# RWKV chunk inverses with exchanged halves on four quadrants, and two LayerNorms centred by the mean of seven tiles ahead of the eighth

## The reference

```python
def _layernorm(x, g, b):
    xf = x.astype(jnp.float32)
    mu = jnp.mean(xf, axis=-1, keepdims=True)
    var = jnp.mean(jnp.square(xf - mu), axis=-1, keepdims=True)
    y = (xf - mu) * lax.rsqrt(var + NORM_EPS) * g.astype(jnp.float32) + b.astype(jnp.float32)
...
    def step(S, inp):
        r_t, w_t, k_t, v_t, a_t, b_t = inp
        sa = jnp.einsum('bhij,bhj->bhi', S, a_t)
        S = S * w_t[:, :, None, :] + sa[..., None] * b_t[:, :, None, :] + v_t[..., None] * k_t[:, :, None, :]
        y = jnp.einsum('bhij,bhj->bhi', S, r_t)
        return S, y
```

## Time and profile before

| | |
|---|---|
| time, median of 3 runs | 2090.66 us (2089.09 to 2099.26) |
| time of the profiled execution | 2087.72 us |
| its span | 2085.9 us |
| PE busy | 1970.8 us (94%), 17574 instructions |
| DVE busy | 1509.0 us (72%) |
| ACT busy | 912.9 us (44%) |
| POOL busy | 516.6 us (25%) |
| RWKV units 0 to 3 begin on PE at | 205.95, 245.13, 294.49, 340.62 us |
| second norm: last residual begins, first scaled tile | 1206.92, 1226.26 us |
| third norm: last residual begins, end of the span | 2062.38, 2085.9 us |

### The profile page before, as it was taken

The page is one execution under the profiler, slowest core; times in us unless marked ns, Lnnn a source line. Parts: engine busy times, 40 slices in busy tenths (PEclk is TensorE's granted clock), DMA queues, the critical chain, the costliest instruction groups (busy, mean ns, idle before and its releaser), DMA issues.

```text
span 2085.9 us, 42823 instructions
## 1 busy us (share of the span) xinstructions
PE 1970.8 (94%) x17574; PEld 1609.5 (77%) x17574; DVE 1509.0 (72%) x2103; ACT 912.9 (44%) x1540; POOL 516.6 (25%) x419
## 2 busy tenths in 40 slices
PE   7999898899999999999999979999989999999997
PEld 6787777777885656655579958888767799999885
DVE  3366665468994677688869866888884789898844
ACT  3325543344324444444465365555443544343423
POOL 2553221140005999300001121111111111111000
PEclk9999999999999999999999989999999999999998
DMA  9222344332452222112138858999964433333321
GB/s 366 86 92 71 124 144 144 145 133 74 157 191 92 71 91 86 61 64 79 66 136 327 294 217 236 311 305 303 323 206 167 142 102 102 103 104 114 137 91 41
DMA packets 127507, 317.89 MB, mean 152 GB/s; under 512 B 12129, under 2 KB 59105, under 8 KB 120913
## 3 DMA queue, kind: packets, MB, share of 16 engines
q1 hardware_dynamic: 114048, 248.65, 35.7%
q0 software_dynamic: 10672, 53.14, 7.0%
q10 hardware_dynamic: 2592, 13.37, 1.6%
HBM read 238.69 MB, written 76.41 MB: 151 GB/s over the span
## 4 chain that ended last, share of the span: by engine, by line
PE 78%; DVE 10%; issue 4%; ACT 4%; DMA 3%; POOL 1%; SPq 1%; ACTq 0%; POOLq 0%; DVEq 0%
PE psum L524 15%; PE psum L3785 14%; PE psum L2017 7%; PE psum L3209 5%; PE psum L2983 5%; PE psum L2640 5%; PE psum L2603 3%; PE psum L1196 3%; PE psum L2615 2%; PE psum L3379 2%; PE psum L337 2%; PE psum L3438 1%; PE psum L3329 1%; PE psum L2691 1%; PE psum L3185 1%
## 5 line engine op out<-in xcount | busy, mean ns | idle before, releaser
L3209 PE MATMUL psum<-h,u_w 128*128 128x256 f32 (+1 forms) x768 | 157.5, 349 | 7.3 <-DVE h L3137 5.2
L524 PE MATMUL psum<-h_split,in_w 128*128 128x512 f32 x600 | 139.1, 391 | 1.5 <-POOL in_w L513 1.5
L3209 PEld LDWEIGHTS psum<-h,u_w 128*128 128x128 f32 x768 | 118.0, 190 | 27.1 <-issue 10.9
L3742 POOL TENSOR_TENSOR ring<-ring 128x1024 f32<-128x1024 f32 x16 | 54.1, 3383 | 319.1 <-DVE xT L3736 319.1
L524 PEld LDWEIGHTS psum<-h_split,in_w 128*128 128x128 f32 x600 | 111.8, 188 | 27.3 <-ACT prev L860 2.1
L513 POOL TENSOR_TENSOR u_w<-ring,u_w 128x512 fp32r<-128x512 f32 x42 | 53.9, 1283 | 276.2 <-ACT u_w L501 240.9
L506 DVE TENSOR_TENSOR w_split<-ring,w_split 128x512 fp32r<-128x512 f32 x54 | 40.4, 748 | 86.3 <-ACT w_split L501 85.9
L2017 PE MATMUL psum<-x_high,ring_split 128*128 128x512 f32 x272 | 101.1, 393 | 0.0
L2640 PE MATMUL psum<-area,ckv_tm 128*128 128x512 f32 (+1 forms) x256 | 100.4, 545 | 0.0
L2738 DVE TENSOR_REDUCE early<-psum 128x1 f32<-128x768 f32 (+1 forms) x96 | 74.8, 780 | 32.2 <-PE psum L2615 29.6
L513 POOL TENSOR_TENSOR in_w<-ring,in_w 128x512 fp32r<-128x512 f32 x50 | 77.4, 1548 | 79.2 <-ACT in_w L501 77.0
(11 more groups left out here) (530 smaller groups left out, 5247.0 us busy)
## 6 DMA issues: line engine op xcount, KB each, us to landing
ring<-in_s_glu SPq DMA_DIRECT2D x64, 512.0 KB, 3.3
ring<-in_w_mod SPq DMA_DIRECT2D x48, 512.0 KB, 5.4
c_pow<-made_c_pow SPq DMA_DIRECT2D x32, 576.0 KB, 5.1
ring<-in_s_in SPq DMA_DIRECT2D x32, 512.0 KB, 6.7
b_pow<-made_b_pow SPq DMA_DIRECT2D x15, 1024.0 KB, 10.5
ring<-in_w_in SPq DMA_DIRECT2D x25, 512.0 KB, 3.3
table<-made_table SPq DMA_DIRECT2D x32, 384.0 KB, 6.6
made_c_pow<-area POOLq DMA_DIRECT2D x10, 1152.0 KB, 5.7
```

Of the source, the lines that this page charges most:

```text
L524: ins = nc.tensor.matmul(out, rounded(buffer(u, w)[:, ks]), values(x, k), start=(first and k == 0 and n == 0), stop=(last and k == UNIT_K ...
L3209: ins = nc.tensor.matmul(o, rounded(u_w[:, u % 4, w, kk * P:(kk + 1) * P]), h3_part(x, k)[:, a:a + size], start=(k == 0 and n == 0), stop= ...
L3742: nc.gpsimd.tensor_tensor(left_plain(i, "S3"), left_plain(i, "A11"), left_plain(i, "S3"), ALU.subtract).then_inc(pool_done, 1)
```

## The change

Two parts. In RWKV, `Z` and `AT` (and so `AL`) are kept with the halves exchanged: the products that make them go to half `1 - odd`. `U` then comes out in the natural half, the step of `Z` in the exchanged half and the step of `ZT` in the natural one, and `dz_pe` issues the two in pairs instead of one after the other. `X(e)` and `Y(e)` become banks `2e` and `2e + 1`. `ZT` no longer comes from `AT`: a new product `at_natural_pe` makes the matrix once more in the natural half, and `zt0_dve` masks it out of PSUM. `akt_pe`, which uses the same bank, follows when that mask is done. At level 2 ACT copies `UA` in two instructions instead of one.

In `ln2` and `ln3` the mean of tiles 0 to 6 (`first_mean_pe`) is formed inside the last tile's products, tiles 0 to 6 are centred by it and squared ahead of tile 7, and tile 7 is centred by it too. What is left of the mean is then the sum of the centred tile 7 over 1024 (`rest`), so the variance is the mean square less the square of `rest`, and each tile gets `rest` subtracted (`rest_dve`, `rest_pool`, "whole") ahead of its scaling. For `ln2` DVE does all 8, for `ln3` GpSimd does two. The first S5 projection of tile 0 multiplies the high part with both weights before it waits for the low part.

```diff
+            def first_mean_pe(self, pe):
+                pe.wait_ge(*at(self.name, "z_sum", KD - 3))
+                self.ones_product(self.mean_bank, self.stat[:, 1, :], True, False)
+                pe.wait_ge(*at(self.name, "z", KD - 2))
+                self.ones_product(self.mean_bank, self.z[:, KD - 2, :], False, True).then_inc(pe_done, 1)
+                pe_count.up(self.name, "first_mean")
...
+            def last_var_pe(self, pe):
+                pe.wait_ge(*at(self.name, "centred", KD - 1))
+                self.quarters_pe(self.rest_bank, self.z[:, KD - 1, :], True, True).then_inc(pe_done, 1)
+                pe_count.up(self.name, "rest_quarters")
+                self.ones_product(self.mean_bank, self.z[:, KD - 1, :], True, True).then_inc(pe_done, 1)
+                pe_count.up(self.name, "rest")
+                pe.wait_ge(*at(self.name, "sq", KD - 1))
+                self.quarters_pe(self.var_bank, self.sq[:, KD - 1, :], False, True).then_inc(pe_done, 1)
+                pe_count.up(self.name, "var")
...
+            def rest_dve(self, dve, k):
+                dve.wait_ge(*at(self.name, "rest_kept"))
+                nc.vector.tensor_tensor(self.z[:, k, :], self.z[:, k, :], self.rest, ALU.add).then_inc(dve_done, 1)
+                dve.wait_ge(dve_done, dve_count.up(self.name, "whole", k))
...
         def X(e, a=0, n=TT * CHUNK):
-            return bank(e, a, a + n)
+            return bank(2 * e, a, a + n)
 
         def Y(e, a=0, n=TT * CHUNK):
-            return bank(2 + e, a, a + n)
+            return bank(2 * e + 1, a, a + n)
...
-                product_pe(b, 0, lhs, rhs).then_inc(pe_done, 1)
+                product_pe(b, 0, lhs, rhs, crossed=True).then_inc(pe_done, 1)
...
+        def at_natural_pe(pe, q):
             for e in range(2):
                 pe.wait_ge(*at("rw", q, "Z0", e))
                 pe.wait_ge(*at("rw", q, "RBT_masked", e))
+            product_pe(0, 0, b_cm, a_cm).then_inc(pe_done, 1)
+            pe_count.up("rw", q, "AT_natural")
+
+        def akt_pe(pe, q):
+            for e in range(2):
+                pe.wait_ge(*at("rw", q, "ZT_masked", e))
             product_pe(0, 0, k_cm, a_cm).then_inc(pe_done, 1)
...
-                if level < LEVELS:
-                    turns(e, 0, lambda h, tt: ZZ[h, 1, tt, :], lambda h, tt: UA[h, 0, tt, :])
-                turns(e, 256, lambda h, tt: UA[h, 0, tt, :], lambda h, tt: ZZ[h, 1, tt, :]).then_inc(pe_done, 1)
+                for tt in range(TT):
+                    if level < LEVELS:
+                        crossed_turn(2 * e, 0, tt, lambda h, tt: ZZ[h, 1, tt, :], lambda h, tt: UA[h, 0, tt, :])
+                    ins = turn(2 * e + 1, 256, tt, lambda h, tt: UA[h, 0, tt, :], lambda h, tt: ZZ[h, 1, tt, :])
+                ins.then_inc(pe_done, 1)
...
-            akt_pe(pe, i)
+            at_natural_pe(pe, i)
             if scan:
                 state_pe(pe, i - 1, 1)
+            akt_pe(pe, i)
...
-            for m in range(1, KD):
+            for m in range(1, KD - 1):
                 mla_out_steps_pe(pe, m, 0, KE)
+            mla_out_steps_pe(pe, KD - 1, 0, KD)
+            ln2.first_mean_pe(pe)
+            mla_out_steps_pe(pe, KD - 1, KD, KE)
...
                 ln2.scale_dve(dve, k)
                 if k == 2:
                     lags_dve(dve, 0)
+                if k + 3 < KD:
+                    ln2.rest_dve(dve, k + 3)
...
+                    if m == KD - 1 and unit == 1:
+                        ln3.first_mean_pe(pe)
```

More of the change, by code:

```diff
@@ L364, in build, with __init__ @@
         class LayerNorm:
-            def __init__(self, name, z, tokens, sq, stat, gain, shift, eps_col, mean_bank, var_bank):
+            def __init__(self, name, z, tokens, sq, stat, gain, shift, eps_col, mean_bank, var_bank, rest_bank=None, rest=None, by_pool=0):
                 self.name, self.z, self.tokens, self.sq, self.stat = name, z, tokens, sq, stat
@@ L403, in mean_pe, with quarters_pe, first_var_pe @@
                 pe_count.up(self.name, "mean")
+            def first_mean_pe(self, pe):
[4 more added lines that the diff above has]
+                pe_count.up(self.name, "first_mean")
+            def quarters_pe(self, b, src, start, stop):
+                for q in range(4):
+                    ins = nc.tensor.matmul(bank(b, 0, self.quarter)[32 * q:32 * q + 32, :], mask("ones")[:, 0:32],
+                                           src[:, self.quarter_of(q)], start=start, stop=stop)
+                return ins
+            def first_var_pe(self, pe):
+                for k in range(KD - 1):
+                    pe.wait_ge(*at(self.name, "sq", k))
+                    self.quarters_pe(self.var_bank, self.sq[:, k, :], k == 0, False)
+            def last_var_pe(self, pe):
[7 more added lines that the diff above has]
+                pe_count.up(self.name, "var")
             def var_pe(self, pe):
@@ L418, in spread_pe @@
                 pe.wait_ge(*at(self.name, "rate"))
+                if self.rest is not None:
+                    pe.wait_ge(*at(self.name, "rest_kept"))
                 edge = self.tokens - T
@@ L456, in scale_dve @@
             def scale_dve(self, dve, k):
+                if self.rest is not None and k >= KD - self.by_pool:
+                    dve.wait_ge(*at(self.name, "whole", k))
                 if k in (0, KD - 1):
@@ L1282, in u_act_ @@
                 if level == 2:
[L1283 to L1286, removed]
+                    nc.scalar.activation(unit["UA", e][:, 1, :, :], tt4(X(e, 256)), ACT.Copy).then_inc(act_done, 1)
+                    act_count.up()
+                nc.scalar.activation(unit["UA", e][:, 0, :, :], tt4(Y(e)), ACT.Copy).then_inc(act_done, 1)
                 act.wait_ge(act_done, act_count.up("rw", q, ("U_copied", level), e))
@@ L1323, in zt0_dve @@
             v = nc.vector
+            dve.wait_ge(*at("rw", q, "AT_natural"))
+            for e in range(2):
+                v.tensor_tensor(unit["ZZ", e][:, 1, :, :], tt4(X(e)), over(mask("diag2_upper"), TT), ALU.mult).then_inc(dve_done, 1)
+                dve_count.up("rw", q, "ZT_masked", e)
             for e in range(2):
@@ L1329, in zt0_dve @@
                 ZT = unit["ZZ", e][:, 1, :, :]
[L1330 to L1331 removed]
+                dve.wait_ge(*at("rw", q, "ZT_masked", e))
                 v.tensor_tensor(ZT, ZT, over(mask("dup")[:, 0:CHUNK], TT), ALU.add).then_inc(dve_done, 1)
@@ L3990, in ln3_dve @@
         def ln3_dve(dve):
-            ln3.centre_dve(dve)
+            ln3.variance_dve(dve)
             ln3.rate_dve(dve)
+            for k in range(3):
+                ln3.rest_dve(dve, k)
             for k in range(KD):
                 ln3.scale_dve(dve, k)
+                if k % 2 == 0 and k + 6 < 2 * (KD - 2):
+                    ln3.rest_dve(dve, 3 + k // 2)
         gl.close()
@@ L4230, in _ @@
             mla_out_dve(dve)
-            ln2.centre_dve(dve)
+            ln2.variance_dve(dve)
             phase_end(dve, dve_count, "mla")
             ln2.rate_dve(dve)
+            for k in range(3):
+                ln2.rest_dve(dve, k)
             s5_start_dve(dve)
```

119 lines of the change are left out of this document (93 added, 26 removed).

## The result

The changed kernel takes 2100.98 us (median of 15 runs, 2096.73 to 2105.76) where the kernel before takes 2090.06 beside it (15 runs): ratio 1.0047, 95% interval 1.0035 to 1.0058, so 7 to 12 us slower. I had forecast 5.7 us less. The profiled execution of the changed kernel has a span of 2099.4 us, 13.5 more than before.

What follows compares the result with a forecast made beforehand. TensorE was taken as the bound, 78% of the chain. RWKV -9.0 (-14.9 + 2.6 + 1.8 + 1.5), second norm +4.3, third -1.0 sum to -5.7: 2090.66 becomes 2085.0 us, range 2076.5 to 2092.

Steps and rivals of the forecast that it cites:

- In the second: Second norm: 4.3 us slower, or 2.2 without the collision of DVE and GpSimd; bounds +1 to +5.
- the three additions: Second norm: three additions of `rest` before the first scaling take 1.9 to 2.0 each beside GpSimd, spending the root's gain.
- the five in the loop: Second norm: five turns of DVE's loop each get an addition of 0.98, 4.9 in all, of which 0.6 fills gaps.
- tile 7's scaling, the row that I had named: Second norm, sign to look for: tile 7's scaling some 4.3 us later against the first scaling.
- In the third: Third norm: 1.0 us faster; 3.1 faster without collision, 0 if GpSimd's additions end last.
- gain: RWKV levels 1 to 4: four quadrants instead of two save 14.9 us of PE; bounds 0 to 14.9.
- The Trainium skill's rule: RWKV: different row tiles cannot access one PSUM bank at once; by it the 14.9 us term would be 0.
- new product and its masks: RWKV: 0.47 us a unit plus mask waits; about 1.5 in unit 0, 1.0 in unit 1; 2.6 in sum.
- Last, the instruction queue ... I put 1.5 on that (0 to 6): RWKV: the same instructions in less time meet the issue pieces harder, costing 1.5 us, bounds 0 to 6.
- Instruction supply bounds RWKV: Rival: RWKV's saving turns into longer issue pieces, 6.0 to 7.5 us back, about +1 in all, 2091.5; chance 0.08.
- PE's clock ... which I cost at nothing: Caveat, cost 0: the forecast is wrong altogether if PE's clock or weight streams elsewhere shift with the earlier start.
- where I had 2.5: RWKV waits: the part of the 2.6 us costs beyond 1.9 of products, plus 1.8 from PE reaching its next waits sooner.

Runs made afterwards that it cites:

- the long run: The kernel before plus 512 back-to-back 64 by 64 products in four quadrants ahead of unit 0's products in RWKV: 2122.95 us, beside 2087.84.
- The filler: 16 overwritten 128 by 256 products ahead of the steps of levels 1 to 4: ratio 1.0030 on the RWKV part alone, 1.0012 on the kernel before.
- the wait that turned into issue: RWKV part alone, with TensorE's vector rows moved between the new product and the product that waits for its mask: ratio 1.0038.
- the three paces with one time: RWKV part alone with steps in pairs, in pairs at levels 1 and 2 only, or one after the other: +8.2, +7.5, +9.0 us.
- alone: The kernel before with only the RWKV part of the change, the norms as they were: ratio 1.0039, +8.2 us.
- in blocks: RWKV part alone, but a level's two steps one after the other in two quadrants each; exchanged halves and new product stay: ratio 1.0043, +9.0 us.

## Why the prediction was wrong

The norms came out as worked. In the second, 4.1 for 4.3: the root gained about 1.1, the three additions spent it (5.23; I had 1.9 to 2.0 each), the five in the loop cost 4.3. That 4.1 meets 4.3 so closely is in part luck: tile 7's scaling, the row that I had named, begins 4.9 later (at 1260.51 instead of 1245.27, less RWKV's 10.3), and the rest of S5 gives 0.8 back, which I had not worked out. In the third, 0.9 for 1.0.

In RWKV the **gain** was right: 64 records in 1.09 us instead of 2.01 at the full clock, 14.7 us for my 14.9. The Trainium skill's rule, page "TensorEngine Tiling (Array Packing)", section "Restrictions and Gotchas", did not show in these 1.09 us, though each row half writes both banks at once. The **new product and its masks** were right too: 0.47 and waits of 1.03, 0.91, 0.46 and 0.47.

The step that failed is "Last, the instruction queue ... I put 1.5 on that (0 to 6)". In the two traces the issue pieces grew by 12.1 us, twice my upper bound. I read the packets' size and the issue pieces (some eight of up to 1.73; the trace has nine, of up to 1.78), but I never set the pace of the products against that of the packets. The earlier trace rows and the queue's row would have allowed it: 128 records with their loads are one packet of 16.4 KB, and four quadrants use it up in 2.1 us. Eight issue pieces in a stretch whose densest work is half as fast were the sign that packets do not come that often. My rival "Instruction supply bounds RWKV" was the right mechanism, with a price too small and a chance of 0.08; the sign that I gave for it, 64 records in 1.1 us and more issue time, is what came.

The second failure is "PE's clock ... which I cost at nothing". In the changed kernel the clock is lower, 0.92 for 0.96 on average in RWKV, which is worth up to 8.5 us, and four of its drops stand right behind long issue pieces. So the budget of the profiled execution is: -14.9 pace, +1.9 new products, +8.6 clock (not measured by itself, but what is left of the busy time's -4.4), +14.0 idle time (12.1 of it issue; the other 1.9 are waits for other engines, where I had 2.5), in sum +9.6.

That issue pieces are waits for blocks is shown in the long run, where they recur at every 128 records, and within RWKV by the packets themselves. For the piece from 267.31 to 270.33 the view of the DMA queues of the changed kernel has, from 264 to 268 us,

```profile
q1 hardware_dynamic: 389, 1.41, 100.4%
```

and from 268 to 269

```profile
q1 hardware_dynamic: 57, 0.17, 44.3%
q8 instruction: 1, 0.02, 6.0%
```

and no other packet of the instruction queue until PE goes on. This one landed at 269.01, and PE went on 1.3 us later. So it is with every piece: all 14 issue pieces of the changed kernel and all nine of the kernel before end 1.2 to 1.6 us after such a packet landed, in the long run 1.2 to 1.5. PE's waits for DVE in the changed kernel end anywhere from 0.4 to 8.4 us after one. The filler, the wait that turned into issue and the three paces with one time agree with it.

The Trainium skill, page "Runtime: NRT & Kernel Launch", section "Instruction fetch mechanics", has blocks of 256 instructions, with which the 8 packets agree. It also says that fetching stays hidden, because instructions are issued more slowly than blocks come in. The waits of 1.63 to 1.91 contradict that, and the measurement decides.

That one pair of traces has luck in it shows in the other runs. With the old RWKV four profiled executions (the kernel before, the norms alone, the third norm alone, the norms without loop additions) have a mean clock of 0.96, 0.94, 0.91 and 0.94 in it; five with the new (as changed, alone, in blocks, rows under the mask, filler) have 0.92, 0.89, 0.90, 0.89 and 0.92. The four take 192.73, 196.96, 199.40 and 193.93 us for RWKV, with issue pieces of 8.3 to 9.3 us; the three in pairs without filler take 202.36, 203.48 and 203.65, with 18.3 to 21.4. So the growth of issue time holds in every trace, and RWKV is 7.4 longer on average where the pair above has 9.6; the timed +8.2 is the number to trust.

**Open:** why RWKV's pieces reach 3.61 us where the long run never waits more than 1.91; no run was made for that. For the four longest (2.34, 3.02, 3.15 and 3.61) the packet starts only 0.05 to 1.25 us after PE has stopped, where it starts 0.4 to 1.0 before ahead of the six waits of 1.63 to 1.91 in the long run; in the 3 us ahead of that start the DMA engines are at 0.85 to 1.00, in the long run at 0.02. That other transfers hold the block back is likely but not shown, since shorter pieces have engines as full ahead of them. Open too is how much of the clock's fall the issue pieces cause, since the clock also falls in places in every trace of the old RWKV.

## What to carry to other kernels

Before making small matmuls denser, divide: how many instructions does the new stretch issue in a microsecond, and how many arrive? Here 256 arrive in 3.7 to 4.0 us in a long dense stretch, and two quadrants of 64x64 fp32 products use just that; past it, a faster pace or a filled wait bought nothing, and a few wide products beside it cost little or nothing. The division has to be made for the dense stretch and not for the stage: all of RWKV needs 40 packets in 202 us, one in 5. An issue piece that ends a fixed time after a packet of the instruction queue has landed (1.2 to 1.6 us here) is a bound, not noise.

Where two engines share work on tensors in SBUF, cost every added two-operand instruction at its price beside the other engine: 1.74 here (5.23 for three) instead of 0.96, and the other engine's four took 7.10 instead of 5.32.

## What was not expected of the hardware

Consecutive blocks that use different pairs of quadrants overlap by themselves: 64 records in blocks took some 1.5 us with exchanged halves where 2.0 were needed when all blocks used the same two.

Four of the five issue pieces of 2 to 3.6 us on TensorE in the changed kernel were followed by 3 to 7 us at a granted clock of half (1.2 GHz); the fifth was not. Up to half of such a stretch is lost, so by an estimate from these lengths a wait cost up to twice its own.

The time from the landing of a packet of instructions to TensorE's next record was 1.2 to 1.6 us at all 23 issue pieces of the two traces, with idle and with full DMA engines.
